# Seven block products instead of eight for the value projection of a decoder step

## The reference, cut to what matters

```python
h = rmsnorm(x, norm_pre1) * (1 + sc1[:, None]) + sh1[:, None]
proj = h @ w_in
split_idx = [int(s) for s in np.cumsum(IN_SIZES)[:-1]]
bg, cg, ua, q, k, v, r, lr, ga, gb = jnp.split(proj, split_idx, axis=-1)
...
v = v.reshape(Bn, T, GLA_HEADS, GLA_DV)
```

## Time and profile before

| | before |
|---|---|
| median of 3 runs | 996.61 us (996.41 to 996.63) |
| span of the profiled execution | 999.7 us |
| TensorE busy, share of the span | 981.8 us, 98% |
| VectorE busy | 553.3 us, 55% |
| ScalarE busy | 386.1 us, 39% |
| GpSimd busy | 221.8 us, 22% |
| TensorE in the chain that ended last | 97% |

### The profile page before, as it was taken

How to read it: one execution, slowest core, us unless ns; L and a number is a source line. 1 busy time by engine, 2 the same in 40 slices (tenths; PEclk the granted TensorE clock), 3 DMA queues, 4 the chain that set the end, 5 groups by cost and what they waited for, 6 DMA issues and landing times.

```text
span 999.7 us, 18680 instructions
## 1 busy us (share of the span) xinstructions
PE 981.8 (98%) x7719; PEld 894.0 (89%) x7719; DVE 553.3 (55%) x884; ACT 386.1 (39%) x593; POOL 221.8 (22%) x121
## 2 busy tenths in 40 slices
PE   6999999998999999999999999999999999999997
PEld 5889889988999999999998799999999999888886
DVE  2511105575765564436438688777777778760204
ACT  4545333324343333443563345333333334533212
POOL 3043533143343343223343000000000000003430
PEclk9999999999999999999999999999999999999999
DMA  9765344796555757536437043222223222422212
GB/s 325 227 112 172 119 72 112 138 116 125 162 128 155 146 129 134 101 95 162 122 99 213 1 127 86 64 85 85 86 85 85 85 86 64 127 85 85 81 54 94
DMA packets 145028, 115.59 MB, mean 116 GB/s; under 512 B 11225, under 2 KB 121585, under 8 KB 144945
## 3 DMA queue, kind: packets, MB, share of 16 engines
q1 hardware_dynamic: 144849, 114.38, 43.8%
q10 hardware_dynamic: 96, 0.04, 0.0%
HBM read 107.02 MB, written 7.35 MB: 114 GB/s over the span
## 4 chain that ended last, share of the span: by engine, by line
PE 97%; DVE 1%; DMA 1%; ACT 1%; issue 0%; SPq 0%; DVEq 0%; ACTq 0%
PE pair L1974 51%; PE pair L2080 16%; PE pair L2395 10%; PE pair L2348 5%; PE pair L1964 2%; PE pair L2161 1%; PE pair L2134 1%; PE pair L1904 1%; DMA x_tok<-in_x_prompt 1%; PE pair L2072 1%; PE pair L2213 1%; PE pair L2224 1%; PE pair L2073 1%; PE pair L2074 1%; PE pair L2071 1%; PE pair L1916 1%
## 5 line engine op out<-in xcount | busy, mean ns | idle before, releaser
L1974 PE MATMUL pair<-h_hi,w_hi 128*128 128x288 f32 x1264 | 283.1, 301 | 0.1
L1974 PE MATMUL pair<-h_hi,w_lo 128*128 128x288 f32 x1264 | 276.2, 296 | 0.3 <-issue 0.3
L1974 PE MATMUL pair<-h_lo,w_hi 128*128 128x288 f32 x1264 | 276.0, 296 | 0.0
L893 POOL TENSOR_TENSOR w_lo<-raw,w_hi 128x1024 fp32r<-128x1024 f32 x53 | 129.0, 2435 | 556.1 <-ACT w_hi L968 556.1
L1974 PEld LDWEIGHTS pair<-h_hi,w_hi 128*128 128x128 f32 x1264 | 205.2, 189 | 18.4 <-issue 16.7
L1974 PEld LDWEIGHTS pair<-h_hi,w_lo 128*128 128x128 f32 x1264 | 205.6, 189 | 0.5 <-issue 0.5
L1974 PEld LDWEIGHTS pair<-h_lo,w_hi 128*128 128x128 f32 x1264 | 205.8, 189 | 0.0
L968 ACT ACTIVATE w_hi<-raw 128x1024 fp32r<-128x1024 f32 x66 | 69.5, 1057 | 162.2 <-PE pair L2074 81.1
L893 POOL TENSOR_TENSOR w_lo<-raw_c,w_hi 128x1024 fp32r<-128x1024 f32 x24 | 69.7, 2909 | 125.8 <-ACT w_hi L968 125.8
L2080 PE MATMUL pair<-w_hi,f_hi 128*128 128x512 f32 x176 | 68.8, 391 | 0.0
L2080 PE MATMUL pair<-w_lo,f_hi 128*128 128x512 f32 x176 | 68.7, 390 | 0.0
(11 more groups left out here) (351 smaller groups left out, 1618.9 us busy)
## 6 DMA issues: line engine op xcount, KB each, us to landing
raw_c<-in_w_ada SPq DMA_DIRECT2D x32, 512.0 KB, 5.4
raw<-in_w_in SPq DMA_DIRECT2D x224, 64.0 KB, 3.1
raw_c<-in_w_in SPq DMA_DIRECT2D x192, 64.0 KB, 3.6
raw<-in_w_up SPq DMA_DIRECT2D x24, 512.0 KB, 4.8
raw<-in_w_down SPq DMA_DIRECT2D x22, 512.0 KB, 3.8
raw_up<-in_w_up SPq DMA_DIRECT2D x20, 512.0 KB, 3.8
ada_first<-in_w_ada SPq DMA_DIRECT2D x16, 512.0 KB, 9.7
raw<-in_w_in SPq DMA_DIRECT2D x8, 512.0 KB, 5.0
```

What stands on the lines that cost most here:

```text
L893: pool.tensor_tensor(lo, raw_tile(n)[:, :], hi.bitcast(F32), ALU.subtract).then_inc(S("w_lo_done"), 1)
L1974: ins = pe.matmul(bank[pair][:, half, 0:HALF], w[:, i, :], x[:, i, HALF * half:HALF * half + HALF], start=i == 0 and p == 0, stop=i == KT ...
```

## The change

The prompt's value product is written as two by two blocks: tokens (A1, A2: 256 each) by weight rows (512 each) on one side, weight rows by columns (B11, B12, B21, B22) on the other. Winograd's form of Strassen's scheme gets it from seven block products, with four sums of token blocks (`s_32`, split into `s_hi` and `s_lo`) and four sums of weight blocks:

T1 = B12 - B11, T2 = B22 - T1, T3 = B22 - B12, T4 = B21 - T2.

Each block product takes two weight tiles, so there are 16 tiles (`m` = 0 to 15) in the order B11, B21, T1, T2, B22, T3, B12, T4. B12 has no product for the prompt: its two tiles serve the samples alone, which are multiplied with the plain blocks as before. A tile has 12 matmuls for the prompt and, for B11, B21, B22 and B12, four for the samples.

- ScalarE makes the high parts of all 16 tiles, of the four token sums, and copies products out of PSUM.
- GpSimd makes the low parts of the eight plain tiles.
- VectorE makes the token sums and their low parts, the weight sums (in place, in the raw buffers), the low parts of the eight tiles of sums, and adds products in `v_tok`.
- SP loads all four blocks ahead of the stage, into `raw0`, `raw1` and the six `raw_c`; the loads for the next stage and for the modulation wait for the raw buffers to come free.
- VectorE's clearing of `score` moves behind the stage.

```diff
+B11, B21, T1, T2, B22, T3, B12, T4 = range(8)
+V_X, V_V, V_W, V_SMP = 2, 1, 0, 3
 ...
 SP
-            for n in range(8):
-                load_raw(TILE_V + n, v_w[n % 4, :, :, 512 * (n // 4):512 * (n // 4) + 512])
-                if n < 2:
-                    load_c1(TILE_C1 + 2 + n)
-                elif n < 6:
-                    load_ada(n - 2)
+            sp.wait_ge(S("w_lo_done"), 4)
+            for kind in (B21, B11, B12, B22):
+                load_v(kind)
 ...
+            sp.wait_ge(S("v_sum"), v_sums(T4) + 2)
             for n in (TILE_C1, TILE_C1 + 1):
                 load_c1(n)
+            sp.wait_ge(S("w_lo_done"), TILE_V + 2 * T3 + 2)
+            for x in (2, 3):
+                load_ada(x)
+            for n in (TILE_C1 + 2, TILE_C1 + 3):
+                load_c1(n)
+            for x in range(2):
+                sp.wait_ge(S("w_lo_done"), TILE_V + 2 * T4 + x + 1)
+                load_ada(x)
 GpSimd
+            for m in (0, 1, 2, 3, 8, 9, 12, 13):
+                if m in (8, 12):
+                    pool.wait_ge(S("w_lo_done"), TILE_V + m)
+                pool.wait_ge(S("w_hi_done"), TILE_V + m + 1)
+                pool.tensor_tensor(w_lo[m % 4][:, :], v_raw(m // 2, m % 2)[:, :], w_hi[m % 4][:, :].bitcast(F32),
+                                   ALU.subtract).then_inc(S("w_lo_done"), 1)
 ScalarE
+            for m in range(16):
+                v_high(m + 3)
+                kind = m // 2
+                if m % 2 == 0 or kind in (T3, B22):
+                    continue
+                act.wait_ge(S("ring_free"), TILE_V + m + 1)
+                if kind == B11:
+                    v_copy(V_X, 0, 0)
+                elif kind == T1:
+                    v_copy(V_W, 2, 1)
 ...
 VectorE
+            for i in range(4):
+                dve.wait_ge(S("h_hi_done"), KT + 2 + i + 1)
+                dve.tensor_tensor(s_lo[i][:, :, :], s_32[i][:, :, :], s_hi[i][:, :, :].bitcast(F32), ALU.subtract) \
+                   .then_inc(S("h_lo_done"), 1)
 ...
+            for m in range(16):
+                if m == 7:
+                    v_add(V_V, 0, 0, 1, 2 * B21 + 1)
+                elif m == 9:
+                    v_samples(0)
+                elif m == 13:
+                    v_add(V_W, 0, 1, 5, 2 * B22 + 1)
+                elif m == 15:
+                    v_add(V_X, 2, 1, 4, 2 * T3 + 1)
+                if m // 2 in (T1, T2, T3, T4):
+                    v_low(m)
+                if m == 3:
+                    v_sum(T1, B12, B11)
+                elif m == 5:
+                    v_sum(T2, B22, T1)
+                    v_sum(T4, B21, T2)
+                elif m == 9:
+                    v_sum(T3, B22, B12)
 TensorE
+            for m in range(16):
+                kind, g = m // 2, m % 2
+                if g == 0:
+                    if kind == B11:
+                        pe.wait_ge(S("kq_done"), 6)
+                    elif kind == B21:
+                        pe.wait_ge(S("kq_done"), 8)
+                    elif kind == T1:
+                        pe.wait_ge(S("h_lo_done"), KT + 1)
+                    elif kind == T2:
+                        pe.wait_ge(S("h_lo_done"), KT + 2)
+                        pe.wait_ge(S("v_done"), 1)
 ...
+                    elif kind == T4:
+                        pe.wait_ge(S("v_summed"), 4)
+                pe.wait_ge(S("w_lo_done"), TILE_V + m + 1)
```

More of the change, by code:

```diff
@@ L66 @@
 TILE_K, TILE_Q, TILE_V = 0, HEADS, 2 * HEADS
-TILE_C1 = TILE_V + 8
+TILE_C1 = TILE_V + 16
 TILE_C2 = TILE_C1 + 4 * KT
@@ L903, in _ @@
             low_of_pair(3)
-            with pool.Fori(1, TILE_C1 // 4) as g:
-                for r in range(4):
-                    low(r, w_hi[r][:, :], w_lo[r][:, :], g * 4 + (r + 1))
+            for r in range(4):
+                low(TILE_Q + r, w_hi[r][:, :], w_lo[r][:, :], TILE_Q + r + 1)
+            for m in (0, 1, 2, 3, 8, 9, 12, 13):
[4 more added lines that the diff above has]
+                                   ALU.subtract).then_inc(S("w_lo_done"), 1)
+            pool.wait_ge(S("w_lo_done"), TILE_C1)
             with pool.Fori(TILE_C1 // 4, TILE_C2 // 4) as g:
@@ L1438, in _ @@
+            dve.memset(score[:, :, :], 0.0).then_inc(S("zeroed"), 1)
+            v_samples(1)
             dve.wait_ge(S("zeroed"), 2)
@@ L2084, in token_tiles, with v_product @@
                 return ins
[L2087 to L2098, removed]
+            def v_product(m, pair, block, xs, tokens, first):
+                wh, wl = (k2(w[m % 4]) for w in (w_hi, w_lo))
+                x_hi, x_lo = xs
+                g = m % 2
+                for x in range(2):
+                    at_ = slice(tokens + P * x, tokens + P * x + P)
+                    for i in range(2):
+                        xh, xl = x_hi[:, block + 2 * g + i, at_], x_lo[:, block + 2 * g + i, at_]
+                        for p, (w, xx) in enumerate(((wh, xh), (wl, xh), (wh, xl))):
+                            ins = pe.matmul(bank[pair][:, x, :], xx, w[:, i, :], start=first and g == i == p == 0,
+                                            stop=g == i == 1 and p == 2, skip_group_check=not first)
+                return ins
@@ new lines, in v_smp_product @@
+            def v_smp_product(m, c, block, first, last):
+                wh, wl = (k2(w[m % 4]) for w in (w_hi, w_lo))
+                g = m % 2
+                dst = bank[V_SMP][:, c, :]
+                one, two = (h_smp_hl[:, block + 2 * g + i, :] for i in range(2))
+                pe.matmul(dst, one, wh[:, 0, :], start=first and g == 0, stop=False)
+                pe.matmul(dst[0:64, :], one[:, 0:64], wl[:, 0, :], start=False, stop=False)
+                pe.matmul(dst[0:64, :], two[:, 0:64], wl[:, 1, :], start=False, stop=False)
+                return pe.matmul(dst, two, wh[:, 1, :], start=False, stop=last and g == 1)
@@ L2099, in _ @@
                         pe.wait_ge(S("stacked"), 2)
+                        pe.wait_ge(S("z_min"), 4)
                         pe.wait_ge(S("prm_done"), 4)
-                    ins = token_tiles(TILE_V + n, n % 4, V_BANK[c], h_hi, h_lo, n % 4 == 0, n % 4 == 3, "v_mm", tiles, h_smp_hl)
+                    ins = v_smp_product(m, 0, 0, True, False)
+                elif kind == B21:
+                    v_product(m, V_V, 4, plain, 0, True)
+                    ins = v_smp_product(m, 0, 4, False, True)
+                elif kind == T1:
+                    ins = v_product(m, V_W, 0, sums[0], 0, True)
+                elif kind == T2:
+                    ins = v_product(m, V_X, 0, sums[1], 0, False)
+                elif kind == B22:
+                    v_product(m, V_W, 0, sums[3], 0, False)
+                    ins = v_smp_product(m, 1, 4, True, False)
+                elif kind == T3:
+                    ins = v_product(m, V_X, 0, sums[2], 0, False)
+                elif kind == B12:
+                    ins = v_smp_product(m, 1, 0, False, True)
+                else:
+                    ins = v_product(m, V_X, 4, plain, 2 * P, False)
```

137 lines of the change are left out of this document (110 added, 27 removed).

## The result

The changed kernel takes 999.55 us (median of 22 runs, 998.02 to 1000.96) where the kernel before takes 996.65 (22 runs, 994.48 to 1000.48). The ratio is 1.0025 with an interval of 1.0016 to 1.0034, that is 2.5 us slower by the ratio, between 1.6 and 3.4 (the medians lie 2.9 apart). The forecast was 999.9 and +3.24. TensorE does 24 matmuls less and the kernel is slower.

The account below looks back on a forecast made before the run. TensorE, busy 98% of the span, was taken to bound the kernel. -5.47 + 1.78 + 4.79 + 2.14 = +3.24 us on 996.61 gave 999.9 us, range 997.0 to 1002.6.

Parts of the forecast that it names:

- The 5.47 us removed: Value projection on TensorE: 24 matmuls fewer at 0.2278 us spacing, 5.47 us off, the whole possible gain.
- The fourth tile, 1.78: TensorE waits 1.78 us at 101.71 for GpSimd's low part of the fourth weight tile.
- T1, 4.79: TensorE waits 4.79 us for T1, behind VectorE's queue after the logarithm; T1 starts at 111.93.
- rival 2: VectorE's subtractions run at the one-operand rate, 0.75 us for 1.22, or a shorter chain otherwise: 994.7 us; chance 0.06.
- T2, 2.14, and the clock: T2 waits 2.14 us for VectorE's low part, swallowing the 1.6 us that T1 probably loses to half clock.
- The rest: From T2 to the stage's end: no waits (1.4 us at most), 112 matmuls, 25.51 us, ending at 145.05.
- Rival 1: Value stage: clock or engine locks cost up to 2.7 or 1.4 us more, 1001.3 to 1002.6 us; chance 0.12.
- rival 3: Unexplained 2.72 us TensorE wait is in plain runs too: moved into cover, 995.7 (0.07), or new one arises, 1004.1 (0.05).
- The profile against the runs: Whole kernel: profiled span 3.1 us above the median of 996.61, carried over to a span of about 1002.9.

Follow-up runs that it names:

- e6: Changed kernel with token-sum low parts, T1 and T2 sums and fourth high part before the logarithm, subtraction and clearings after T3's low parts; 989.63 us, ratio 0.9942.
- e1: Changed kernel with T2's first low part put ahead of T4's two sums on VectorE; 998.70 us, ratio 1.0025 to the kernel before.
- b2: The kernel before, unchanged, run again for a second profile; 996.36 us (1 run).
- e2: Changed kernel with the four low parts of the token sums moved ahead of VectorE's wait for the logarithm; 994.27 us, ratio 0.9989 to the kernel before.
- e7: e6 plus six VectorE clearings of an unused buffer ahead of T1's first low part; 995.17 us, ratio 0.9992 to the kernel before.
- e9_wait7: e6 plus seven VectorE clearings of an unused buffer ahead of T1's first low part; 997.17 us (1 run).

## Why the prediction was right, and where it was not

- **The 5.47 us removed.** Right, and it is the whole gain: 5.46 in e6, where nothing waits.
- **The fourth tile, 1.78.** 1.55 in the row; from the matmul before (101.11) to this one 1.93, less one spacing, 1.70. GpSimd's low part took 3.79 for the 3.83 of the earlier trace rows.
- **T1, 4.79.** 4.50 in the row, 4.65 from start to start less a spacing. Forecast for T1's start was 21.15 us behind the projection's first matmul (111.93 - 90.78); it is 21.12 (111.47 - 90.35). Sums and low parts on VectorE are 1.13 apart (2.35 for two, 3.49 for three), as the earlier trace rows had it, so rival 2 (0.75 us each) falls.
- **T2, 2.14, and the clock.** VectorE is ready when forecast: T2 starts 28.66 us behind the first matmul, forecast 28.76. Of the 2.14 the trace shows 0.25 as a wait, because T1's half-rate matmuls took 1.66 us more (118.60 - 111.47 = 7.13 for 5.47). The prediction had said 1.6 and that T2's wait swallows it; e1, where T2 waits for nothing and the stage is no shorter, agrees. It did not say the reverse, that T2's wait is worth nothing as long as T1's clock falls.
- **The rest.** No wait from T2 on, spacing 0.228; the stage 54.25 us, forecast 145.05 - 90.78 = 54.27. That these agree to 0.02 is in part luck: from start to start the three waits, with T1's slow matmuls in the last, come to 1.70 + 4.65 + 2.07 = 8.42 for 8.71, and 0.27 of wider spacing, mostly just behind the waits, which the sum had at nothing, makes up for it. Rival 1 (locks and clock cost more than their cover) did not come, and TensorE's list of waits in the changed kernel has no unexplained one as in rival 3.
- **The profile against the runs.** Here a step was wrong. I set the span of 999.7 against the median of 996.61 and took 3.1 us for the surplus of that execution, so I expected a span of 1002.9 for the changed kernel; it is 997.5. A run's time is 1.7 us above its span (b2: 996.36 and 994.6; changed: 999.23 and 997.5), so the surplus was 4.8, and the span after had to be counted without it. The reason that I gave, a wait that most plain runs lack, fits b2, which has none. The forecast of the time carried only the difference over, and so was not touched.
- **What I missed in the experiments** is that the clock's loss is hidden or open depending on what waits next. In e2's profile it came into the open and took 1.6 of the 4.5 us. In e7 I expected the clock to fall, and in the profiled execution it did not.

## What to carry to other kernels

A product saved on a bound engine is worth its spacing, but only if what prepares the next product stands early in another engine's queue: look for the point behind which that engine works without a gap (here the logarithm), and move ahead of it all that doesn't need it. Waits on one chain aren't terms to be removed one by one; the longest downstream one sets the price, the ones ahead of it are free until it is gone, and slow matmuls behind it can lie beside the next wait. A wait of some microseconds on TensorE should be priced with the half-rate matmuls that may stand behind it, 1.6 to 2.5 us here, unless the next wait hides them. And one profile is one execution: where its clock differs from that of the plain runs, it tells the mechanism but not the median.

## What the runs showed of the hardware

- TensorE's clock, in one execution each: full behind a single wait of 3.31 us, half behind one of 4.49 and behind one of 1.84 that followed a 1.55. In the changed kernel it was still granted in full at the end of the 4.5 us wait and fell some 0.4 us into T1; in e9_wait7 it was half already when T1 began.
- VectorE's two-operand subtractions and GpSimd's run one behind the other: e6's two sums at 87.25 take 4.54 us for 2.35 while a low part on GpSimd, at 86.19, takes 3.39 for 2.40. The clearing of suf does not hold GpSimd up: in the changed kernel its low part of 99.20 ends at 102.99 while the clearing runs from 101.31 to 103.29. Nor does VectorE's addition of PSUM onto SBUF. In e6, the addition and the low part run at their usual lengths side by side:

```profile
123.54 1.21 DVE L1544 TENSOR_TENSOR v_tok<-v_tok,pair 128x1024 f32<-128x1024 f32 x1
...
123.89 2.40 POOL L950 TENSOR_TENSOR w_lo<-raw_c,w_hi 128x1024 fp32r<-128x1024 f32 x1 [0.53 <-ACT w_hi L1087]
```
